# A two-layer diffusion backbone step: q and kv tiles between the first state space products, their norms in the z stage, gates one tile ahead of outputs

## What is computed

```python
def token_mixing(h, lw, ctx):
    proj = h @ lw["w_in"]              # z | xbc | dt | q_down | kv_down | f_in
    ...
    q = (rms_norm(q_down, lw["g_q_norm"]) @ lw["w_q_up"]).reshape(...)
    ckv = rms_norm(kv_down[..., :KV_LORA], lw["g_kv_norm"])
    ...
    o_mla = mla_attend(q_nope, q_pe, keys_ckv, keys_kpe, lw["w_kv_up"]) @ lw["w_mla_out"]
    o_ssd, h_final = ssd_branch(z, xbc, dt_raw, h0, lw)
    o_fft = fourier_branch(f_in) @ lw["w_fft_out"]
    gates = jax.nn.sigmoid(h @ lw["w_gate"] + lw["b_gate"])
    g_ssd, g_mla, g_fft = jnp.split(gates, N_BRANCH, axis=-1)
    out = (g_ssd * o_ssd + g_mla * o_mla + g_fft * o_fft) @ lw["w_o"]

def ssd_branch(z, xbc, dt_raw, h0, lw):
    xbc = jax.nn.silu(dwconv_centred(xbc, lw["conv_ssd_w"], lw["conv_ssd_b"]))
    dt = jax.nn.softplus(dt_raw + lw["dt_bias"])
    ...                                # chunked scan forwards and backwards
    y = rms_norm(y * jax.nn.silu(z), lw["g_ssd_norm"])
    return y @ lw["w_ssd_out"], h_final
```

## Time and profile before

| | |
|---|---|
| median of 3 runs | 2017.85 us (2013.92 to 2020.84) |
| the profiled execution | 2018.73 us, its span 2017.0 us |
| mean granted clock of TensorE | 0.968 of full speed |
| busy time | PE 1824.6 us (90%), DVE 1106.7 (55%), ACT 883.7 (44%), POOL 35.8 (2%) |
| layer 0: `proj`, to `z`, `z`, `out_ssd` | 52 to 131, to 229.3, to 262.8, to 340 us from the span's start |
| layer 1, the same | 1032 to 1112.6, to 1210.5, to 1245, to 1324 us |

### The profile page before, as it was taken

One profiled execution on the slowest core, in us unless ns is written; L12 is line 12 of the kernel. 1 busy time (PEld: TensorE's weight loads), 2 busy tenths in 40 slices (PEclk: granted clock), 3 DMA queues, 4 the chain that ended last, 5 costly groups with the idle time before them and its releaser, 6 DMA issues.

```text
span 2017.0 us, 32134 instructions
## 1 busy us (share of the span) xinstructions
PE 1824.6 (90%) x11178; PEld 1669.2 (83%) x11178; DVE 1106.7 (55%) x1801; ACT 883.7 (44%) x1532; POOL 35.8 (2%) x58
## 2 busy tenths in 40 slices
PE   4986989889999989999989688988999997999995
PEld 2974889669999789999969368977799996999994
DVE  1657554664334577367365665356542447754754
ACT  2543543663343454244354354256533345443432
POOL 1000000000000000000000000000000000000000
PEclk9988999999999999999989899999999999999998
DMA  7320223223343623434533103331233453333331
GB/s 301 136 97 21 84 97 122 74 84 113 125 152 128 254 84 125 158 124 145 217 117 125 45 2 125 116 124 57 78 125 105 172 201 139 127 114 125 125 114 62
DMA packets 56319, 244.08 MB, mean 121 GB/s; under 512 B 6368, under 2 KB 6448, under 8 KB 52624
## 3 DMA queue, kind: packets, MB, share of 16 engines
q1 hardware_dynamic: 49824, 181.43, 26.7%
q0 software_dynamic: 6384, 61.19, 7.7%
HBM read 238.63 MB, written 3.96 MB: 120 GB/s over the span
## 4 chain that ended last, share of the span: by engine, by line
PE 64%; issue 21%; DVE 8%; ACT 5%; DMA 1%; DVEq 0%; ACTq 0%; POOL 0%; SPq 0%; POOLq 0%
PE ps L1228 18%; PE ps L1230 17%; PE ps L1229 17%; DVE rstd L1684 1%; PE ps L580 1%; PE ps L609 1%; PE ps L1304 1%; PE ps L643 1%; ACT region L785 1%; PE ps L1275 1%; PE ps L595 1%; PE ps L489 1%; PE ps L517 1%; ACT w_hi L1424 1%; DMA raw<-in_weights 1%
## 5 line engine op out<-in xcount | busy, mean ns | idle before, releaser
L1424 ACT ACTIVATE w_hi<-raw 128x1024 fp32r<-128x1024 f32 x344 | 364.5, 1060 | 688.0 <-PE ps L1230 687.1
L1228 PE MATMUL ps<-h_hi,w_hi 128*128 128x384 f32 x1632 | 557.4, 342 | 28.2 <-DVE h_lo L1676 27.3
L1229 PE MATMUL ps<-h_lo,w_hi 128*128 128x384 f32 x1632 | 552.4, 338 | 0.0
L1230 PE MATMUL ps<-h_hi,w_lo 128*128 128x384 f32 x1632 | 552.1, 338 | 0.0
L1672 DVE TENSOR_TENSOR w_lo<-raw,w_hi 128x1024 fp32r<-128x1024 f32 x248 | 303.9, 1225 | 351.6 <-ACT w_hi L1424 309.3
L1228 PE MATMUL ps<-in_hi,w_hi 128*128 128x384 f32 x992 | 341.1, 344 | 25.7 <-DVE in_lo L860 7.8
L1228 PEld LDWEIGHTS ps<-h_hi,w_hi 128*128 128x128 f32 x1632 | 308.3, 189 | 38.6 <-DVE h_lo L1676 20.6
L1229 PE MATMUL ps<-in_lo,w_hi 128*128 128x384 f32 x992 | 337.5, 340 | 0.0
L1230 PE MATMUL ps<-in_hi,w_lo 128*128 128x384 f32 x992 | 337.4, 340 | 0.0
L1229 PEld LDWEIGHTS ps<-h_lo,w_hi 128*128 128x128 f32 x1632 | 309.3, 190 | 0.3
L1230 PEld LDWEIGHTS ps<-h_hi,w_lo 128*128 128x128 f32 x1632 | 309.1, 189 | 0.0
(11 more groups left out here) (237 smaller groups left out, 1738.1 us busy)
## 6 DMA issues: line engine op xcount, KB each, us to landing
raw<-in_weights SPq DMA_DIRECT2D x346, 512.0 KB, 3.2
region<-in_ada POOLq DMA_DIRECT2D x18, 2048.0 KB, 11.4
mix<-in_ada POOLq DMA_DIRECT2D x2, 1536.0 KB, 23.2
wide<-in_ada POOLq DMA_DIRECT2D x2, 1536.0 KB, 7.1
region<-in_ada POOLq DMA_DIRECT2D x2, 1536.0 KB, 7.2
region<-in_state POOLq DMA_DIRECT2D x2, 1024.0 KB, 5.1
region<-in_ada POOLq DMA_DIRECT2D x4, 512.0 KB, 8.5
out_state<-wide POOLq DMA_DIRECT2D x4, 512.0 KB, 3.0
```

The lines of the kernel that those rows point to most:

```text
L1228: pe.matmul(out, ah, bh, start=start, stop=False)
L1229: pe.matmul(out, ah, bl, start=False, stop=False)
L1230: m = pe.matmul(out, al, bh, start=False, stop=stop)
L1424: act.activation(w_hi[:, j % AHEAD, :], raw[:, nxt, :], ACT.Copy).then_inc(hi_made.sem, 1)
```

## The change

1. The dt and rotary key tile comes first in `proj`. `dt_turn`, `dt_magnitude`, the two parts of `step_sizes` and `cumulated` follow the convolution tiles (counted from 0) 1, 2, 3 and 4, and 6; `cumulate` stands before TensorE's tile 6, `side` 4 before tile 11.
2. The two kv and three q tiles (`late_tile`) go to TensorE between the transposes, the chunk states and the products of C and B, in other banks; `late_take` and `late_refill` do their part on VectorE and ScalarE. Their values stay raw, kv in `ckv`, q in three places of `region`.
3. The squares, sums, roots, reciprocals, scalings and high and low parts of kv and q lie in and right behind the z stage, before z tiles 2 to 6 and after the last. GpSimd's copy of the rotary keys and the storing of ckv wait for them.
4. `out_ssd` runs gate 0, gate 1, output 0, gate 2, output 1, ..., gate 7, output 6, output 7, with two gate buffers. The weights of its third tile are prepared amid the high parts (ScalarE) and before the low parts (VectorE).
5. The wait for the third modulation vector stands before head tile 2 instead of head tile 0.

```diff
@@ PE, state space part
-        TOKEN_ORDER = [(2, 0), (0, 3), (1, 0)]
+        TOKEN_ORDER = [(2, 3), (0, 0), (1, 3)]
+        LATE_BANKS = (1, 7, 6, 7, 6)
...
+            late_tile(0)
+            pe.wait_ge(silu_done.sem, silu_done.at(L, 10))
+            pe.wait_ge(rows_out.sem, rows_out.at(L, 5))
+            pe.wait_ge(taken.sem, taken.at(L, STAGES["proj"][0] + 12 + AHEAD))
+            turn_tokens(0)
+            late_tile(1)
+            pe.wait_ge(taken.sem, taken.at(L, STAGES["proj"][0] + 14 + AHEAD))
+            turn_tokens(1)
             pe.wait_ge(dt_exp.sem, dt_exp.at(L, 2))
...
+            late_tile(2)
+            pe.wait_ge(tok_ready.sem, tok_ready.at(L, 1))
+            turn_tokens(2)
+            late_tile(3)
...
-            for n in range(4):
-                state(n)
-            for n in range(4):
+            state(0)
+            chunk_products()
+            state(1)
+            late_tile(4)
+            state(2)
+            state(3)
+            entering(0)
+            pe.wait_ge(taken.sem, taken.at(L, STAGES["proj"][0] + 18 + AHEAD))
+            for n in range(1, 4):
                 entering(n)
@@ PE, stages
-                project(L, "proj", h_hi, h_lo, (h_lo_made, h_lo_made.at(L, 1)), banks=4)
-                dt_turn(pe, L)
-                norm_sum(L, 2, mix[:, KVB + QB:, :])
-                side(L, 4)
-                norm_sum(L, 3, mix[:, KVB + QB:, :])
-                ssd(pe, L)
+                tile_in(L, t0)
+                tile_product(t0, 0, h_hi, h_lo, (h_lo_made, h_lo_made.at(L, 1)), 4)
+                def conv_tile(t, turn, j, k):
+                    if isinstance(k, int) and k == 1:
+                        dt_turn(pe, L)
+                    if isinstance(k, int) and k == 6:
+                        cumulate(pe, L)
+                    if isinstance(k, int) and k == XBC_B - 1:
+                        side(L, 4)
...
-                project(L, "z", h_hi, h_lo)
+                def z_tile(t, turn, j, k):
+                    if k == 2:
+                        norm_sum(L, 2, latent_squares)
+                        norm_sum(L, 3, latent_squares[:, KVB:, :], bank=5)
...
-                pe.wait_ge(cols_taken.sem, cols_taken.at(L, 3))
                 def tile(half, i):
+                    if half == 0 and i == 2:
+                        pe.wait_ge(cols_taken.sem, cols_taken.at(L, 3))
@@ ACT, convolution tile k
+                    if isinstance(k, int) and k == 3:
+                        act.wait_ge(dt_abs.sem, dt_abs.at(L, 1))
+                        act.activation(dts[:, 3, :], dts[:, 2, :], ACT.Exp, scale=-1.0)
+                        act.activation(dts[:, 4, 0:32], param("a_log", 0, 32), ACT.Exp).then_inc(dt_exp.sem, 1)
                     refill(L, t, turn, j)
@@ DVE, convolution tiles and late tiles
+                    split(L, t, turn, j)
+                    taps(L, k, j, "conv_w", k, None)
+                    if isinstance(k, int):
+                        if k == 2:
+                            dt_magnitude(L, dve, link)
+                        elif k == 3:
+                            step_sizes(L, dve, link, 0)
+                        elif k == 4:
+                            step_sizes(L, dve, link, 1)
+                        elif k == 6:
+                            cumulated(L, dve, link)
...
+                def late_take(i):
+                    t = t0 + 1 + XBC_B + i
+                    into = ckv[:, i, 0:T] if i < KVB else q_raw[i - KVB]
                     dve.wait_ge(used.sem, used.at(L, t + 1))
+                    dve.tensor_copy(into, ps[:, LATE_BANKS[i], 0:T]).then_inc(taken.sem, 1)
+                    split(L, t, t // RING, t % RING)
@@ DVE, z tile k and after
+                    if k == 2:
+                        norm(L, 2)
+                    elif k == 3:
+                        for i in range(KVB):
+                            link(L, dve.scalar_tensor_tensor(out=ckv[:, i, 0:T], in0=ckv[:, i, 0:T], scalar=param("g_kv", i),
+                                                             in1=rstd[:, :], op0=ALU.mult, op1=ALU.mult))
...
+                    elif k == 4:
+                        dve.wait_ge(roots.sem, roots.at(L, 3))
+                        link(L, dve.reciprocal(rstd[:, :], gated[:, :]))
...
+                t = STAGES["out_ssd"][0]
+                split(L, t, t // RING, t % RING)
                 y_los(L, 0, lambda k: wide[:, k, :])
-                merge(L, "out_ssd", 0)
+                ssd_merge(L, split)
@@ DVE, gated stage: the new function, a gate tile
+                if is_gate:
+                    if not (isinstance(k, int) and k == 0):
+                        low_weight(L, t, turn, j)
+                    dve.wait_ge(gate_made.sem, gate_made.at(L, i + 1))
+                    after(dve).then_inc(taken.sem, 1)
+                    return
@@ POOL
-                pool.wait_ge(y_added.sem, y_added.at(L, 2 * CHUNKS))
+                pool.wait_ge(ckv_ready.sem, ckv_ready.at(L, 1))
+                settle(pool, pool_marks)
+                pool.dma_start(o_ckv[L], ckv[:, :, 0:CTX]).then_inc(stored, 16)
+                pool.wait_ge(kvq_lo_made.sem, kvq_lo_made.at(L, 5))
                 pool.wait_ge(kpe_ready.sem, kpe_ready.at(L, 3))
```

More of the change, by code:

```diff
@@ L156, in build_program @@
         kpe = sb("kpe", [96, KEYS])
-        low = mix[:, 0:KVB + QB, :]
         ckv = sb("ckv", [P, KVB, KEYS])
@@ L730, in gates, with staggered, place, one @@
             pairs(act, stage, body)
+        def staggered(eng, stage, body):
+            first, count = STAGES[stage]
+            end = first + count
+            def place(n):
+                if n == 0 or (n % 2 and n < count - 1):
+                    return (n + 1) // 2, True
+                return (n // 2 - 1 if n < count - 1 else count // 2 - 1), False
+            def one(t):
+                i, is_gate = place(t - first)
+                body(t, t // RING, t % RING, t - first, i, is_gate, gate_of[i % 2])
+            t = first
+            while t % RING or t - first < RING:
+                one(t)
+                t += 1
+            turns = (end - 1 - t) // RING
+            with eng.Fori(0, turns) as r:
+                for j in range(RING):
+                    i, is_gate = place(t + j - first)
+                    body(r * RING + (t + j), r + t // RING, j, r * RING + (t + j - first), r * (RING // 2) + i, is_gate,
+                         gate_of[i % 2])
+            t += turns * RING
+            while t < end:
+                one(t)
+                t += 1
         def pairs(eng, stage, body):
```

281 lines of the change are left out of this document (161 added, 120 removed).

## The result

The changed kernel takes 1996.44 us (median of 4 runs, 1995.14 to 2000.11) and the kernel before, beside it, 2018.12 us (2013.92 to 2020.84): ratio 0.9892, 95% interval 0.9873 to 0.9911, so 21.7 us or 1.1% faster. Run again on another occasion it had the ratio 0.9886 [0.9865, 0.9907]. The profiled execution took 1996.11 us with a span of 1994.3. The forecast was 2000.0 with a range of 1990 to 2013, faster with 0.79.

A forecast was written before the change was run, and what follows sets the result against it. TensorE's matmuls plus its waits and slow clock were taken as the bound. Layer 0: 12.7 - 4.4 - 2.2 + 2.4 = 8.5 us, layer 1: 10.0, together 18.5 off 2018.7, so 2000; range 1990 to 2013.

The forecast's parts named there:

- B: z stage: takes over the norm blocks and norm work, losing 4.4 us per layer.
- C: Head of the first gated stage: one wait replaces another and GpSimd's copy delays scalings, losing 2.2 us per layer.
- A: Projection stage and state space start: three waits and slow clock go, a cumulation wait comes; 12.7 us gained per layer.
- D: End of the gated stage: the third modulation vector's wait is covered, gaining 2.4 us in layer 0, 3.9 in layer 1.
- Rival 2: Convolution and z tiles: VectorE becomes the bound in both stages, slower at 2037 us; chance 0.09.
- rival 1: After the new waits the clock stays up and GpSimd's copy disturbs nothing: 9 us more gain, 1991; chance 0.15.
- Rival 3: Small operations and table loads take twice the room, cumulate waits 10 us: about no change, 2011.2 or 2013; chance 0.14.

The follow-up runs named there:

- the two kernels without it: Changed kernel with the cumulation moved to convolution tile 11, 1994.7 us; the same with step sizes in four pieces, ratio 0.9826.
- the first eight experiments: Edits to the changed kernel: cumulation late, also step sizes spread, modulation wait back, pairs, copy early, mark early, x_end first, all together; 1973.6 us for the last.
- the one with step sizes spread: Changed kernel with the cumulation at the last convolution tile and step sizes in four pieces behind tiles 3 to 6; ratio 0.9826.
- the kernel with x_end first: Changed kernel with x_end of state 3 made on VectorE ahead of the last late tile's copy and w_lo; ratio 0.9881.
- the execution with the modulation wait: Changed kernel with the wait for the third modulation vector back ahead of head tile 0; 2006.4 us.
- the one in pairs: Changed kernel with gate and branch tiles of the first gated stage in pairs again; ratio 0.1 to 0.2% more than the changed kernel.

## Why the prediction was right

The time fell by 21.7 us, 18.5 were forecast; the mechanism was the one forecast, and the sizes of its terms were off by up to 2 us a layer. How closely B and C come out in one layer is in part luck, since the clock behind the same wait differs from one execution to the next by about 1 us.

- **A, the three waits and the slow clock beside them against one wait at the cumulation.** Right: 13.1 and 13.7 gained for 12.7. The wait was 4.51 and 4.59 us, not 5.2. VectorE wrote dt_ready at 90.37, as forecast (90.4); TensorE came later, at 85.9 and not 85.3: from the first tile's end (59.97, as forecast) the six convolution tiles with the dt transposes took 25.9 us and not 25.3. The clock behind it cost 6.6 x 0.44 = 2.9 and 6.6 x 0.35 = 2.3 (2.5 forecast). The wait ahead of the first transposes was 0.56 (1.0), state 3's 1.82 (1.9). That the wait and the clock are one cause is shown by the two kernels without it.
- **B, the norms in the z stage.** Right in the sum: -4.7 and -3.6 us for -4.4. The five norm blocks took 3.4 us (3.6). The waits for w_lo and the later last squares (0.8 in the sum) did not come: the added sum waited 1.64 us in either kernel. Of the rest, 0.9 us in layer 0 is the first z tile's clock: 1.00 before and 0.79 after, against 0.82 and 0.84 in layer 1, behind the same 1.8 us wait. That is chance: the changed kernel run again had 1.00 in both layers, and B was -4.0 and -3.0. Rival 2 (VectorE is the bound in both tile stages) fell with it: no tile of the z stage waited over 0.04 us for w_lo.
- **C, the head.** The mis-sized term. From gate 0's start, three tiles took 18.7 and 19.7 us before, 19.9 and 19.8 after: -1.2 and -0.1, where -2.2 was forecast. GpSimd's copy cost 0.8 us and not 1.5, since it started 0.2 and not 0.6 after the low parts, and so reached less far into the scalings; and the wait was 5.13 and not 5.8. The 0.5 for a lower clock behind the longer wait rests on a price that the rows don't give: the clock was 0.73 here against 0.72 in the earlier trace rows, but 0.57 and 0.55 when the changed kernel was run again, where the head took 20.7 and 20.9 us (-2.0 and -1.2). So the small loss in C is in part luck. In layer 1 branch 0 had been slower before (6.9 us, at a clock of 0.55 behind the same 3.9 us wait), which the forecast, made from layer 0, did not have.
  The Trainium skill (SBUF — State Buffer, Who interferes with whom), by which the scalings, with two SBUF inputs, are caught and the one-input reciprocal isn't, agrees with the trace: 5.13 against 4.33 us for the scalings with and without the copy beside them, 2.55 for the reciprocal in both.
- **D.** Right: the wait of 2.4 us is gone in both layers, and putting it back cost 7 to 8 us in all, 6.3 forecast. By layer the rest gained 1.1 and 5.8 us for 2.4 and 3.9; it is 690 us long, so the difference can't be put down to D.
- **The rivals.** Of rival 1, half came true: the copy cost little, the clock did not stay up. Rival 3 (a wait of 10 us) did not come: the chained operations took what the earlier trace rows say.

In the trace, 22.9 us came where 18.5 were forecast: 1.4 more in A, 3.1 in B and C, 0.6 in the rest with D, 0.7 less between entering states and z. Of the 3.1, the head of layer 1 is 2.1 (-0.1 for -2.2), the head of layer 0 1.0, and B 0.5; tiles of 4.24 us instead of 4.17 in layer 0's gated stage took some of it back.

## What to carry to other kernels

When small chained work is moved beside a saturated engine, count what the helper has left per tile and how far ahead its product is wanted, then cut the work to pieces of that size and let the consumer wait last: here pieces of 2 us and a later matmul gave as much again as half of the change. A mark or semaphore that costs nothing must not stand behind work that the waiting engine doesn't need; until it is moved, any reordering on the waiting engine only trades one wait for another. Price the wait and the clock behind it together, and take the price from several rows for that length of wait, as a range: one row each, as in this forecast, made a price look exact that differs by over 1 us between executions.

## What the hardware showed that was not expected

**The clock after a wait is not settled by the wait.** Ahead of the last row products before the z stage TensorE waits 1.8 us in every kernel and layer here, after sparse work. In ten profiles (before, after and the first eight experiments, two layers each) the first 4.2 us of the z stage had a granted clock of 1.00 six times, 0.74 to 0.85 eleven times and 0.59 three times. In the eleven the low clock had begun in the last row products already (0.91 to 0.95 over the 12 us before z, 1.00 in the other nine). Both parts together cost 1.6 to 1.7 us in each of the fourteen, so this is one price that is paid or not, and not a scale. Equal code in layer 0 and layer 1 of one execution differed (the kernel with x_end first, table by stretch):

```profile
216.20:220.40 4.20, 4.20 (x26) 4.18 (x25) 0.69 (x1) 0.00 (x0) 1.06 (x2) 1.00 0.37 82
1188.70:1192.90 4.20, 4.20 (x17) 4.17 (x16) 0.69 (x1) 0.00 (x0) 1.06 (x2) 0.59 0.40 89
```

After waits of 0.6 and 1.65 us in mid-stage it stayed at 1.00, and after 2.4 it was 1.00 twice and 0.63 and 0.70 once each. After 3.9 to 5.8 us it was always low, but by how much differed more between executions than with the length of the wait: over 6.0 us in the branch product 0.52 to 0.76, behind waits of 5.1 us alone. The table by stretch has the changed kernel run again (5.2 us), then the kernel before in layer 1 (3.9 us), then the one with step sizes spread, layers 0 and 1 (5.1 us):

```profile
272.20:278.20 6.00, 5.99 (x21) 6.00 (x22) 0.89 (x1) 0.38 (x1) 0.00 (x0) 0.57 0.27 87
1257.80:1263.80 6.00, 5.98 (x20) 5.98 (x21) 4.38 (x8) 3.13 (x5) 0.00 (x0) 0.55 0.08 17
265.60:271.60 6.00, 6.00 (x19) 6.00 (x20) 0.88 (x1) 0.37 (x1) 0.00 (x0) 0.52 0.27 87
1231.00:1237.00 6.00, 6.00 (x27) 6.00 (x28) 1.07 (x2) 0.57 (x2) 0.00 (x0) 0.76 0.27 90
```

The branch product, 4.5 us at full clock, took 5.6 to 6.9 us behind such waits. Behind the cumulation's wait (4.4 to 4.6 us) the clock was 0.51 to 0.66 over 6.6 us.

**Tiles of 24 matmuls differ by 2% at a granted clock of 1.00.** In the gated stage of layer 0 a tile began 4.16 us after the one before in the execution with the modulation wait, 4.24 in the one in pairs. It is not a property of an execution either: in layer 1 the one in pairs had 4.16, and the kernel before had 4.16 in layer 0's projection stage and 4.24 in layer 1's. The table by line of the stretch from 286 to 333 us has it in the mean too, 335 and 338 ns for one. First the execution with the modulation wait:

```profile
L1314 PE MATMUL ps<-in_hi,w_hi 128*128 128x384 f32 x51 | 17.1, 335 | 0.0
```

then the one in pairs:

```profile
L1312 PE MATMUL ps<-in_hi,w_hi 128*128 128x384 f32 x42 | 14.2, 338 | 0.0
```

The table by stretch has the same clock in both, first for the modulation wait:

```profile
286.00:333.00 47.00, 47.00 (x273) 47.00 (x272) 16.80 (x17) 14.01 (x16) 0.00 (x0) 1.00 0.37 124
```

and for the pairs:

```profile
286.00:333.00 47.00, 47.00 (x268) 47.00 (x268) 16.80 (x17) 14.01 (x16) 0.00 (x0) 1.00 0.37 124
```

Over a whole execution that is several microseconds in stages that no edit touches, as large as some of the edits here; its cause stays open. Experiments of under 0.3% were therefore read by stretch and not by their time.
